# Gate blocks of the first and the last attention layer, moved against the projections and the second attention call

## The reference

```python
def modulation(cvec, w_ada, b_ada):
    return jnp.split(jax.nn.silu(cvec) @ w_ada + b_ada, 3, axis=-1)
...
        sh_l, sc_l, gt_l = modulation(c, w_ada, b_ada)
        sh_c, sc_c, gt_c = modulation(c_ctx, w_ada, b_ada)
        h_l = rmsnorm(x_lat, g_pre) * (1.0 + sc_l[:, None, :]) + sh_l[:, None, :]
        h_c = rmsnorm(x_ctx, g_pre) * (1.0 + sc_c) + sh_c
        y_l, y_c = mixer(h_l, h_c, need_ctx=need_ctx)
        x_lat = x_lat + gt_l[:, None, :] * rmsnorm(y_l, g_post)
```

## Time and profile before

| | us |
|---|---|
| median of 3 runs | 1559.55 |
| fastest, slowest | 1559.46, 1567.86 |
| profiled execution | 1564.55 |
| span of its instructions | 1562.7 |
| TensorE busy in the span | 1469.1 |
| VectorE busy | 993.5 |
| ScalarE busy | 754.6 |
| mean granted clock of TensorE | 0.98 |

### The profile page before, as it was taken

How to read it: one execution, slowest core, us unless ns; L and a number is a source line. 1 busy time by engine, 2 the same in 40 slices (tenths; PEclk the granted TensorE clock), 3 DMA queues, 4 the chain that set the end, 5 groups by cost and what they waited for, 6 DMA issues and landing times.

```text
span 1562.7 us, 24142 instructions
## 1 busy us (share of the span) xinstructions
PE 1469.1 (94%) x9392; PEld 1204.4 (77%) x9392; DVE 993.5 (64%) x2286; ACT 754.6 (48%) x1630; POOL 67.5 (4%) x76
## 2 busy tenths in 40 slices
PE   6999999999999999999979999897999899999999
PEld 4777766777778777888757777576787798799987
DVE  4647677565566648535684677666777476777763
ACT  4436566453655443331143555555566347455542
POOL 0000000100000100020010100001101020000000
PEclk9999999999999999999989999899999999999999
DMA  9121180222560332221461253333435542445554
GB/s 362 55 108 55 57 316 21 102 82 67 189 230 1 108 102 81 94 68 54 170 221 54 76 159 102 139 98 126 162 125 155 197 161 95 149 148 189 189 189 135
DMA packets 59866, 202.84 MB, mean 130 GB/s; under 512 B 7694, under 2 KB 10984, under 8 KB 59624
## 3 DMA queue, kind: packets, MB, share of 16 engines
q1 hardware_dynamic: 53568, 192.84, 35.5%
q10 hardware_dynamic: 6008, 7.40, 2.1%
q0 software_dynamic: 176, 1.06, 0.2%
HBM read 199.43 MB, written 1.84 MB: 129 GB/s over the span
## 4 chain that ended last, share of the span: by engine, by line
PE 72%; DVE 15%; ACT 5%; DMA 4%; issue 3%; POOL 1%; SPq 0%; ACTq 0%; POOLq 0%; DVEq 0%
PE ps L2243 66%; PE ps L2246 5%; DVE w_l L2913 3%; DVE st L3012 1%; ACT w_h L2556 1%; DVE l_P L2917 1%; DVE x L2921 1%; DMA w_l_ada<-in_l_ada 1%; DMA w_raw<-in_l_out 1%; DVE m_P L3496 1%; ACT l_P L2559 1%; DVE l_xn L2917 1%; DVE l_h_lat L2921 1%; DMA w_raw<-in_l_ada 1%; POOL mstat L3590 1%
## 5 line engine op out<-in xcount | busy, mean ns | idle before, releaser
L2913 DVE TENSOR_TENSOR w_l<-w_raw,w_h 128x1024 fp32r<-128x1024 f32 (+3 forms) x263 | 315.4, 1206 | 74.9 <-ACT w_h L2556 74.4
L2556 ACT ACTIVATE w_h<-w_raw 128x1024 fp32r<-128x1024 f32 (+3 forms) x263 | 272.1, 1042 | 109.6 <-DMA w_raw<-in_f_down 25.3
L2243 PE MATMUL ps<-w_h,l_hTh 128*128 128x512 f32 (+1 forms) x384 | 156.2, 407 | 0.5 <-DVE w_l L2913 0.4
L2243 PE MATMUL ps<-w_h,l_hTl 128*128 128x512 f32 (+1 forms) x384 | 151.8, 395 | 0.0
L2243 PE MATMUL ps<-w_l,l_hTh 128*128 128x512 f32 (+1 forms) x384 | 151.8, 395 | 0.0
L2559 ACT ACTIVATE l_P<-ps,st 128x512 f32<-128x512 f32 (+1 forms) x128 | 77.6, 608 | 91.5 <-DVE st L2921 64.2
L3012 DVE TENSOR_REDUCE st<-ps 128x1 f32<-128x512 f32 (+2 forms) x112 | 72.7, 649 | 43.9 <-PE ps L2243 43.7
L2243 PE MATMUL ps<-f_hTh,w_h 128*128 128x256 f32 x352 | 99.2, 282 | 0.0
L2243 PE MATMUL ps<-f_hTl,w_h 128*128 128x256 f32 x352 | 99.1, 281 | 0.0
L2243 PE MATMUL ps<-f_hTh,w_l 128*128 128x256 f32 x352 | 99.0, 281 | 0.0
L2243 PE MATMUL ps<-l_hTh,w_h 128*128 128x512 f32 (+1 forms) x264 | 97.5, 369 | 0.5 <-issue 0.5
(11 more groups left out here) (444 smaller groups left out, 3467.9 us busy)
## 6 DMA issues: line engine op xcount, KB each, us to landing
w_raw<-in_l_ada SPq DMA_DIRECT2D x49, 512.0 KB, 5.3
w_raw<-in_l_z SPq DMA_DIRECT2D x32, 512.0 KB, 3.5
w_raw<-in_l_adg SPq DMA_DIRECT2D x32, 512.0 KB, 3.9
w_raw<-in_l_out SPq DMA_DIRECT2D x32, 512.0 KB, 4.7
w_raw<-in_m_merge SPq DMA_DIRECT2D x24, 512.0 KB, 3.3
w_raw<-in_f_gate SPq DMA_DIRECT2D x22, 512.0 KB, 3.3
w_raw<-in_f_up SPq DMA_DIRECT2D x22, 512.0 KB, 3.2
w_raw<-in_f_down SPq DMA_DIRECT2D x22, 512.0 KB, 4.2
```

The lines of the kernel that those rows point to most:

```text
L2243: return p.e.matmul(out, lhsT, rhs, start=start, stop=stop)
L2556: return p.e.activation(out, a, func, scale=scale)
L2913: return p.e.tensor_tensor(out, a, b, op)
```

## The change

In layer 0 the gate's eight blocks are asked for during the first z projection: four pairs, at the fourth, seventh, eleventh and fourteenth of its 16 steps, into a bank of ATT. What is left of the gate (bias, rounding, spreading) is braided with the 16 blocks of layer 1's shift and scale in the second call, at 21 steps for 28. In layer 3 the blocks stay in the second call, one pair at every third step of its first twelve, and the rest of the gate goes step by step with the next ten. In both layers the gate's buffers are named before the z projection and its load of g_post is begun where it was. The gate's spreading takes its banks from PAIR also where its blocks used ATT.

```diff
-def weave(main, other, num, den):
+def along(main, other, num, den):
...
     for _ in main:
...
             next(other, None)
+        yield
     drain(other)
+
+
+def weave(main, other, num, den):
+    drain(along(main, other, num, den))
...
-                wait += [[5 + x, lambda x=x: gate.step(x, pool)] for x in range(5)]
+                wait += [[5 + x, lambda x=x: gate.step(x, PAIR)] for x in range(5)]
...
-        drain(m.z(0, hT, f))
+        gate, post = p.ends(i, base, 97 if i == 3 else 0, len(m.tiles))
+        gate = Gate(p, i, *gate, lambda: m.end)
+        if mix:
+            mod = p.ada(PAIR, [(3, "gate")], gate)
+            drain(m.z(0, hT, f))
+        else:
+            row = p.ada(ATT, [(0, "gate")], gate)
+            mod = braid(row, p.ada(PAIR, [(1, 0), (1, 1)]))
+            weave(m.z(0, hT, f), upto(row, 4), 4, 14)
...
-        f = p.fence()
+        f = m.end = p.fence()
         if mix:
             mix.b_free = f
-        gate, post = p.ends(i, base, 97 if i == 3 else 0, len(m.tiles))
-        groups = [(i, "gate")] if i == 3 else [(0, "gate"), (1, 0), (1, 1)]
+        gate.begin()
...
-        weave(upto(post.tail, steps + 6), p.ada(PAIR, groups, Gate(p, i, *gate, f)), 14, steps)
+        if mix:
+            weave(upto(post.tail, 12), upto(mod, 4), 4, 12)
+            weave(upto(post.tail, steps - 6), mod, 10, 10)
+        else:
+            weave(upto(post.tail, steps + 6), mod, 21, steps + 4)
```

## The result

| kernel | median | lowest to highest | runs |
|---|---|---|---|
| before | 1559.36 us | 1554.47 to 1567.86 | 8 |
| after | 1572.00 us | 1566.37 to 1578.81 | 8 |

The ratio is 1.0075, with a 95% interval of 1.0054 to 1.0096: slower by 8.4 to 15.0 us, and within the 1% that the forecast counted as no change. The profiled execution of after took 1573.16 us (span 1571.3), 8.6 more than that of before. A ratio and its interval are estimated from all executions, so a ratio isn't exactly the quotient of the two medians.

The account below looks back on a forecast made before the run. TensorE, busy 94% of the span, was taken as the bound. Terms 4.0 + 7.25 + 2.9 + 3.4 - 5.2 + 0 - 5.3 = +7.05 us, added to the 1559.55 median, gave 1566.6, rounded to 1567; range 1554 to 1579.

Parts of the forecast that it names:

- the three signs of a wrong forecast: Wrong if z grows under 6 us, layer 3 gains over 9 or under 2, layer 0's clock falls over 10 us.
- pairs in z: Layer 0's z projection: four gate pairs of 1.00 us each enter a stretch without slack, +4.0 us.
- waits in z: Layer 0's z projection: lost lookahead makes TensorE wait 2.75 us three times, one pair hiding 1.00; +7.25 us.
- first block of the second q: Layer 0's second q projection: its first block loses its lookahead and starts late, +2.9 us.
- clock in layer 0: Layer 0, behind the new waits: two stretches of 3.4 us at half clock, +3.4 us.
- second call of layer 0: Layer 0's second call: four pairs and l_ada waits of 1.7 leave, 0.5 given back to VectorE's chain; -5.2 us.
- output splits at the turn: Layer 0's output projection: one subtraction moves from the second call's end to the turn; 0, bounds -1.2 and +1.6 us.
- layer 3's second call: Layer 3: l_adg wait -2.0, half clock behind it -1.7, half clock behind the l_gth wait -1.6; sum -5.3 us.
- The gains are whole: Rival, chance 0.18: layer 3's second call gives 12.1 us, layer 0's 5.7, no half clock; total -3.7, 1556 us.
- The clock falls in layer 0 and stays: Rival, chance 0.12: all four layer 0 waits are followed by 6.8 us at half clock; total +22.95, 1582 us.
- Layer 3 gives nothing: Rival, chance 0.10: layer 3's spreads still wait for l_gth and two subtractions delay the chain; 1571 us.
- the splits make no wait: Rival, chance 0.05: only the pairs move, layer 0's splits cause no wait; total -6.5, 1553 us.

Follow-up runs that it names:

- the lookahead run: Changed kernel with layer 0's first z projection blocks requested with a lookahead of 4 in place of 3: 1563.12 us against 1562.76 before, ratio 0.9991.
- the slower pace: Changed kernel with lookahead 4 in layer 0's z, its second call's remaining work at 14 in 24 steps, not 21 in 28: 1560.37 us, ratio 0.9990.
- the split put back: Changed kernel with lookahead 4 in layer 0's z, output projection's second-block split back before layer 0's softmax tail: 1561.30 us, ratio 0.9997.
- the pairs bunched: Kernel before, with layer 3's gate pairs kept at steps 2 to 5 and what follows them from step 13: 1561.55 us, ratio 0.9993.

## Why the prediction was right, and where it was not

The forecast was 1567 with a range of 1554 to 1579, and that it is a loss within 1%. The median is 1572.0. None of the three signs of a wrong forecast came: z grew by 13.7, layer 3 gained 7.1, and layer 0 had 3.4 us at half clock behind the change. Term by term, in us:

| term | forecast | measured | from |
|---|---|---|---|
| pairs in z | +4.0 | +4.8 | 4 x 1.20, from the lookahead run |
| waits in z | +7.25 | +6.9 | 1.63 + 2.64 + 2.63 |
| first block of the second q | +2.9 | +3.2 | shift from fourth l_zT to second l_P |
| clock in layer 0 | +3.4 | +1.7 | one stretch of 3.4 us at half |
| second call of layer 0 | -5.2 | -3.4 | shift |
| output splits at the turn | 0 | +1.8 | shift |
| layer 3's second call | -5.3 | -7.1 | shift |
| sum | +7.05 | +7.9 | |

The shifts themselves go from +0.88 to +8.19, a change of 7.3 up to layer 3's first l_yg. Other stretches gave back 0.9 (0.4 between the second l_P and the call, 0.5 between the turn and layer 3), and z grew by 13.7 where its three terms make 13.4. That the forecast's 7.05 is so near is in part luck: layer 0's second call and turn were 3.6 worse than forecast, and the other terms together took back most of it.

**The waits in z** came as worked out, place by place: 1.63, 2.64, 2.63 and 2.84 where 1.75, 2.75, 2.75 and 2.9 stood. That the subtraction of a block needed much later becomes the one waited for was read from the trace of before and the new order alone. The run with the lookahead of 4 shows it as a cause: the three waits and the half clock in z are gone, 8.35 us by the landmarks, and 1.1 of the 3.2 at the second q. The other 2.1 there stay, so the forecast's 2.9 for that block isn't the z lookahead alone. That the pair inside a z block was not taken into the gap shows in the second and third wait: both whole, 2.64 and 2.63. The Trainium skill (TensorE: Matmul & The Clock Gate, Step-by-step: what each phase is for) says that matmuls stay in program order, and the trace agrees.

**The pairs** were under-sized: "four pairs of 1.00" took a start-to-start time at a place where another short matmul follows. Between the projection's matmuls a pair costs 1.20, so 4.8 for the four.

**The clock** was over-sized by one stretch, 1.7. Another one, at 57.4, lies ahead of every change.

**The second call** is the term that failed most in its reasoning. The prediction gave back 0.5 for "VectorE's chain". TensorE did lose 4.86 us of work there (43.12 to 38.26 busy) and both waits for l_ada, 1.7. But its idle time rose, from 2.98 to 4.46. In the list of TensorE's waits over that call, before has, beside the 1.7 for l_ada, one row (waited for: us in total, times, longest); after has the three of the second fence:

```profile
PE ps L2243 <- DVE l_ogf L2921: 1.1, 2, 0.8
```

```profile
PE ps L2259 <- DVE l_ogf L2937: 2.1, 2, 1.5
PE ps L2259 <- ACT l_P L2575: 1.2, 2, 0.9
PE ps L2262 <- ACT stage L2572: 0.8, 1, 0.8
```

VectorE has 34.80 us of work in 42.72, as against 35.77 in 46.10: with less to do for TensorE the softmax chain seems to set the length. That is read from the waits; no run here changes it alone. The idle time is a chain of short waits, and the longest, for l_ogf, stayed at the slower pace. **The turn** came out past its bound of +1.6, and the split put back did not win it: where VectorE is that full, the 1.22 us are paid on either side.

**Layer 3** gave 7.1 where 5.3 stood, inside its bounds. The reading of the wait for l_gth held: what it called a queue of two roundings and two subtractions, which "cost there what they cost here", is the 4.5 us that left the middle and the 4.2 that came back behind. The wait for l_adg went, as forecast. The size that failed is that of the first part, which became 6.6 shorter. The forecast had 2.0 for the wait and 1.7 for the half clock behind it there, and took the pairs themselves as neutral. But two of the four now stand where they cost nothing, 2.0 by the 1.00 of the earlier trace rows; this makes 5.7, an estimate, and the other 0.9 stays open. The 1.6 for the half clock behind l_gth isn't shown as a term of its own. What was not seen at all is ScalarE's wait for the load of l_out. In before it is hidden; with the pairs bunched or over 8 steps it holds up the chain.

**The sum and the median.** The traces give +8.6, of which 0.9 was there ahead of the first change. That is within 1.6 of the sum of 7.05. But the medians differ by 12.6, with an interval of 8.4 to 15.0. The step that missed is the last of the sum: "I carry the difference over". The profiled execution of before stood 5.2 us above its median of eight and that of after 1.2, and these 4.0 are the gap between traces and medians. Part of them is the clock. The profiled execution of before had a mean granted clock of 0.980, and the 82 executions of before in the three batches, on other chips, have 0.9825 on average; in them 0.001 of clock goes with 1.0 to 1.2 us. That puts the trace of before 2.5 to 3 us on the slow side, an estimate, while that of after (0.984) is at the mean of its eight. So the true cost is likely above the 8.6 of the traces. The ratios of the two halves measured alone, 1.0088 and 0.9944 (or 0.9959 in its second run), add up to +5 us (or +7), each sum uncertain by over 5, so that they reach into the interval of the whole and don't decide.

**The rivals.** "The gains are whole" did not happen in either layer: layer 3 gave 7.1 and not 12.1, layer 0's call 3.4 and not 5.7. "The clock falls in layer 0 and stays" did not happen: one stretch. "Layer 3 gives nothing" and "the splits make no wait" are refuted by the run with layer 3's change alone and by the four waits.

## What to carry to other kernels

Work that is slipped into a loop which prefetches by counting blocks also moves what is prefetched: read the new order on the engine that prepares the operands, and not only where the added work goes. A small edit of the lookahead was worth 9.5 us by the landmarks here, more than layer 3's whole gain. When two waits end near each other, the shorter is hidden, and comes out when the longer is removed: the load of l_out was hidden before, and with the pairs over 8 steps TensorE waited 3.21 us behind it. An engine that runs in order can be held up by a job for later that waits for its load: spread the loads out first, put the job that needs them behind, and pace both to the loop around them, since too fast (5.2 us) and too slow (3.3 us) each lost part of 7.1.

## What the runs showed of the hardware that was not expected

The same wait does not always bring the clock down. TensorE waits 1.73 us at 56.31 in after and 1.74 at 56.98 in before, for the same thing in the same order; before goes on at full clock and after at 0.51 for 3.4 us:

```profile
57.00:60.40 3.40, 3.36 (x19) 2.76 (x20) 1.77 (x3) 1.90 (x5) 0.00 (x0) 1.00 0.00 0
```

All twelve kernels here have this wait, 1.72 to 1.74 us long, behind the same instructions. In eight of the twelve traces 3.4 us at half clock follow, and before is one of the four without. In the same way the waits of 1.63, 2.63 and 2.84 in layer 0 had no lowered stretch behind them, and the one of 2.64 had; in the trace with layer 0's change alone it is again the second of the four. So a price for the clock behind a wait of 1.6 to 2.9 us is a mean and not a rule. Over the 82 executions of before that these batches hold, the mean granted clock lay between 0.977 and 0.988 and the time went with it: the four with 0.978 or less took 1568.7 us on average, the four with 0.987 or more 1556.7. That is the scatter in which a change of a few microseconds has to be found, and why the landmarks of the traces, which are good to some tenths where the clock doesn't fall, told these kernels apart when their intervals overlapped.
